# The last branch's keys turned and split inside the last attention instead of in the projection ahead of it

## The reference, cut to what matters

```python
for layer in range(DEPTH):
    x = sandwich(x, ..., swiglu, MACARON_WEIGHT)
    x = sandwich(x, ..., mixer, 1.0)
    x = sandwich(x, ..., swiglu, MACARON_WEIGHT)
```

```python
qc, kc, vc, ks, vs, kw, vw, gl, qd, kd, vd = split_cols(h @ w_in, CD_COLS)
o_c = g[:, :, 0] * o_cmp + g[:, :, 1] * o_slc + g[:, :, 2] * o_win
o_d = moba_attention(qd, kd, vd, rel_table[...])   # softmax(q k / 8 + bias by distance) v
return concatenate([o_c, o_d]) @ w_out
```

## Time and profile before

| | us |
|---|---|
| median of 3 runs (965.33 to 965.87) | 965.79 |
| the profiled execution, its own time | 966.07 |
| its span | 964.3 |
| TensorE busy | 957.3 (99%) |
| VectorE busy | 774.7 (80%) |
| ScalarE busy | 498.8 (52%) |
| GpSimd busy | 120.7 (13%) |
| granted TensorE clock | 1.00 in nearly all of the span |

### The profile page before, as it was taken

How to read it: one execution, slowest core, us unless ns; L and a number is a source line. 1 busy time by engine, 2 the same in 40 slices (tenths; PEclk the granted TensorE clock), 3 DMA queues, 4 the chain that set the end, 5 groups by cost and what they waited for, 6 DMA issues and landing times.

```text
span 964.3 us, 13463 instructions
## 1 busy us (share of the span) xinstructions
PE 957.3 (99%) x4670; PEld 810.3 (84%) x4670; DVE 774.7 (80%) x1471; ACT 498.8 (52%) x806; POOL 120.7 (13%) x129
## 2 busy tenths in 40 slices
PE   9999999999999999999999999999999999999997
PEld 8888888899888888888888888888889888888886
DVE  6789888768578988887898888878778588888884
ACT  6535343678464443445635353567667465343432
POOL 1200000166520000000200000022242420000000
PEclk9999999999999999999999999999999999999999
DMA  9875566242755657477085756527650436665631
GB/s 354 303 252 198 194 211 229 66 143 88 236 201 175 225 170 249 140 243 235 23 291 175 231 175 217 218 88 232 252 175 2 154 109 212 224 213 179 202 103 44
DMA packets 122178, 179.20 MB, mean 186 GB/s; under 512 B 3056, under 2 KB 97288, under 8 KB 121876
## 3 DMA queue, kind: packets, MB, share of 16 engines
q1 hardware_dynamic: 118900, 172.52, 53.2%
q10 hardware_dynamic: 2928, 4.98, 1.6%
q0 software_dynamic: 304, 1.09, 0.4%
HBM read 177.49 MB, written 1.09 MB: 185 GB/s over the span
## 4 chain that ended last, share of the span: by engine, by line
PE 97%; DVE 1%; issue 1%; ACT 1%; POOL 0%; DVEq 0%; POOLq 0%; ACTq 0%
PE ps L1329 93%; PE ps L1582 1%; PE ps L1367 1%; PE ps L1716 0%; DVE w_lo L1857 0%; PE ps L1343 0%; DVE down_lo L2354 0%; DVE end_hi L2159 0%; ACT moba_k L1313 0%; ACT logit L1124 0%; ACT gpost L1124 0%; PE ps L1442 0%; DVE down_lo L2150 0%; DVE xn L2165 0%; DVE x L1911 0%
## 5 line engine op out<-in xcount | busy, mean ns | idle before, releaser
L1329 PE MATMUL ps<-w_hi,xt_hi 128*128 128x512 f32 (+3 forms) x912 | 351.5, 388 | 0.0
L1329 PE MATMUL ps<-w_hi,xt_lo 128*128 128x512 f32 (+3 forms) x912 | 349.1, 386 | 0.0
L1329 PE MATMUL ps<-w_lo,xt_hi 128*128 128x512 f32 (+3 forms) x912 | 348.5, 385 | 0.0
L1857 DVE TENSOR_TENSOR w_lo<-raw,w_hi 128x2048 fp32r<-128x2048 f32 (+3 forms) x107 | 234.9, 2234 | 47.7 <-ACT w_hi L931 47.2
L1957 DVE STREAM_TRANSPOSE ps<-h 32x128 f32<-32x128 f32 x624 | 201.4, 323 | 9.2
L931 ACT ACTIVATE w_hi<-raw 128x2048 fp32r<-128x2048 f32 (+3 forms) x110 | 200.0, 1864 | 1.9 <-PE ps L1329 1.6
L1329 PEld LDWEIGHTS ps<-w_hi,xt_lo 128*128 128x128 f32 x912 | 171.4, 188 | 33.5
L1329 PEld LDWEIGHTS ps<-w_lo,xt_hi 128*128 128x128 f32 x912 | 171.6, 188 | 32.6
L1329 PEld LDWEIGHTS ps<-w_hi,xt_hi 128*128 128x128 f32 x912 | 171.3, 188 | 32.4
L1042 ACT ACTIVATE ht_hi<-ps 128x512 fp32r<-128x512 f32 x40 | 23.9, 598 | 285.2 <-DVE ps L1957 283.2
L1329 PE MATMUL ps<-down_hi,ht_hi 128*128 128x512 f32 x320 | 124.8, 390 | 0.0
(11 more groups left out here) (219 smaller groups left out, 843.3 us busy)
## 6 DMA issues: line engine op xcount, KB each, us to landing
raw<-in_l_ffn_wg SPq DMA_DIRECT2D x41, 1024.0 KB, 7.3
raw<-in_l_ffn_wu SPq DMA_DIRECT2D x41, 1024.0 KB, 9.8
raw_down<-in_l_ffn_wd SPq DMA_DIRECT2D x40, 1024.0 KB, 5.0
raw<-in_l_w_in SPq DMA_DIRECT2D x10, 1024.0 KB, 7.1
raw<-in_l_w_out SPq DMA_DIRECT2D x8, 1024.0 KB, 6.2
xn<-in_l_ffn_wd SPq DMA_DIRECT2D x4, 1024.0 KB, 7.3
raw<-in_l_w_in SPq DMA_DIRECT2D x4, 768.0 KB, 6.4
lead<-in_first SPq DMA_DIRECT2D x7, 384.0 KB, 6.1
```

Of the source, the lines that this page charges most:

```text
L1329: return pe.matmul(dst, lhs, rhs, start=start, stop=stop, skip_group_check=True)
L1857: dve.tensor_tensor(part(w_lo), part(raw), part(w_hi).bitcast(F32), ALU.subtract).then_inc(main_lo, 1)
```

## The change

The eight transposes of the keys leave chunk 5 of the projection. Four of them are made in step 14 (job 0) and four in step 18 (job 1), behind the scores of the step and ahead of its other transposes, both jobs in bank 6. Step 14's wait until slc tile 0 has been scaled out of that bank; step 18's wait until both low parts of job 0 have been read from it. ScalarE makes the high parts in steps 15, 16, 19 and 20, VectorE the low parts in steps 16, 17, 20 and 22, each behind the exponent or the logits and ahead of the step's copy. GpSimd adds the first two branches ahead of doubling the keys, and the other two behind. The scores of step 24 wait for the keys of job 0, those of step 28 for job 1. ScalarE's copy of the second tile of the values now comes directly behind the first exponents, and VectorE's scaling of the compressed heads directly behind the first logits. The waits that kept banks 0 and 1 until the keys were read are gone; the values of step 29 wait for the last low part.

```diff
+        KEYS_PE = {14: 0, 18: 1}
+        KEYS_ACT = {15: (0, 0), 16: (0, 1), 19: (1, 0), 20: (1, 1)}
+        KEYS_DVE = {16: (0, 0), 17: (0, 1), 20: (1, 0), 22: (1, 1)}
...
-                       job_base["kvv"]: 1, job_base["kd"]: 0, job_base["kd"] + 1: 1}
+                       job_base["kvv"]: 1, job_base["kd"]: 6, job_base["kd"] + 1: 6}
...
+                    add_branches(0, 2)
                     for i in range(2):
                         for par in range(2):
...
                             pool.wait_ge(moba_hi, 5 + 2 * i + par)
                             pool.tensor_copy(hi[others, :, :], hi[rows, :, :]).then_inc(moba_doubled, 1)
...
-                    add_branches()
+                    add_branches(2, 4)
...
-            for name, part, scale in (("qd", 0, scale_a), ("kd", 1, 1.0)):
-                if name == "kd":
-                    exps_ahead("slc")
...
+            def last_high(name, i, par):
+                job, rows = job_base[name] + i, slice(64 * par, 64 * par + 64)
+                act.wait_ge(t_ready, job + 1)
+                act.activation(moba_slots(i, par)[name == "kd"][rows, :, :], t_bank_two(job)[rows, :, :], ACT.Copy,
+                               scale=scale_a if name == "qd" else 1.0).then_inc(moba_hi, 1)
+            for i in range(2):
+                for par in range(2):
+                    last_high("qd", i, par)
+            exps_ahead("slc")
             project_out(j0 + 10, 4, lambda t: [(val[:, t, :], ps[:, 2 + t, :])], tiles=(1,))
-            exps("slc", ALL_STEPS - LAST_BASE)
+            exps("slc", ALL_STEPS - LAST_BASE, aside={n: lambda at=at: last_high("kd", *at) for n, at in KEYS_ACT.items()})
...
-                    if u == LAST_BASE + 4:
-
-                        pe.wait_ge(t_done, job_base["kd"] + 1)
-                    if (name, t, hh) == ("moba", 0, 0):
-                        pe.wait_ge(moba_doubled, 4)
-                        pe.wait_ge(moba_zeroed, 4)
+                    if name == "moba" and t == 0 and hh % 4 == 0:
+                        pe.wait_ge(t_done, job_base["kd"] + 1 + hh // 4)
+                        pe.wait_ge(moba_doubled, 2 + 2 * (hh // 4))
+                        pe.wait_ge(moba_zeroed, 2 + 2 * (hh // 4))
...
-                        if (name, t, hh) == ("win", 0, 0):
+                        if (name, t, hh) == ("moba", 0, 0):
 
                             pe.wait_ge(t_done, job_base["kd"] + 2)
...
-            def turn_last_keys():
-                pe.wait_ge(cmp_t_done, 2)
-                turn_four("kd", 512)
+            def turn_last_keys(i):
+                pe.wait_ge(head_out, OUT_AT["slc", 0])
+                turn_one_of_four("kd", 512, i)
...
-                    beside={3: scores_ahead, 5: turn_last_keys})
+                    beside={3: scores_ahead})
...
+            def last_low(i, par):
+                rows = slice(64 * par, 64 * par + 64)
+                _, k_hi, k_lo = moba_slots(i, par)
+                dve.wait_ge(moba_hi, 5 + 2 * i + par)
+                ins = dve.tensor_tensor(k_lo[rows, :, :], t_bank_two(job_base["kd"] + i)[rows, :, :],
+                                        k_hi[rows, :, :].bitcast(F32), ALU.subtract)
+                if par == 1:
+                    ins.then_inc(t_done, 1)
...
-                aside={5: lambda: compressed_out(1)})
+                aside={5: lambda: compressed_out(1), **{n: lambda at=at: last_low(*at) for n, at in KEYS_DVE.items()}})
```

More of the change, by code:

```diff
@@ L828, in split_both, with add_branches @@
                 split_low(n)
-            def add_branches():
-                for i, (name, t) in enumerate((("slc", 0), ("win", 0), ("slc", 1), ("win", 1))):
+            def add_branches(first, end):
+                for i in range(first, end):
+                    name, t = (("slc", 0), ("win", 0), ("slc", 1), ("win", 1))[i]
                     pool.wait_ge(head_out, OUT_AT[name, t])
@@ L1355, in turn_two, with turn_one_of_four @@
                            for i in range(2) for t in range(TILES)])
+            def turn_one_of_four(name, at, i):
+                turn_two(job_base[name] + i, lambda t, k: stage[:, t, at + (2 * i + k) * P:at + (2 * i + k + 1) * P])
             def turn_four(name, at):
                 for i in range(2):
-                    turn_two(job_base[name] + i, lambda t, k: stage[:, t, at + (2 * i + k) * P:at + (2 * i + k + 1) * P])
+                    turn_one_of_four(name, at, i)
             def turn_whole(src, t, name, before=lambda k: None):
@@ L1831, in _ @@
                          lambda kt, hh: val[:, kt, hh * HEAD:(hh + 1) * HEAD])},
-                LAST_BASE, ALL_STEPS - LAST_BASE, turned="out1")
+                LAST_BASE, ALL_STEPS - LAST_BASE, turned="out1",
+                aside={n: lambda i=i: turn_last_keys(i) for n, i in KEYS_PE.items()})
             pe.wait_ge(proj_out, OUT["w_in1"][3])
@@ L2339, in _ @@
                  32: lambda: scale("moba", 0, 512), 40: lambda: scale("moba", 1, 512)}, turned="out1",
-                aside={5: lambda: compressed_out(1)})
[L2341 to L2358, removed]
+                aside={5: lambda: compressed_out(1), **{n: lambda at=at: last_low(*at) for n, at in KEYS_DVE.items()}})
+            for i in range(2):
+                for par in range(2):
+                    rows, others = slice(64 * par, 64 * par + 64), slice(64 * (1 - par), 64 * (2 - par))
+                    q, _, _ = moba_slots(i, par)
+                    dve.wait_ge(moba_hi, 1 + 2 * i + par)
+                    ins = dve.scalar_tensor_tensor(q[others, :, :], t_bank_two(job_base["qd"] + i)[rows, :, :], scale_a,
+                                                   q[rows, :, :].bitcast(F32), ALU.mult, ALU.subtract)
+                ins.then_inc(t_done, 1)
+            dve.wait_ge(bias_landed, 16)
+            dve.wait_ge(d_lo, 6 * FBLOCKS)
+            first_last()
             compressed_out(0)
```

## The result

The changed kernel takes 968.18 us (median of 10 executions, 967.72 to 968.48) against 965.82 for the one before (10 executions beside it). The ratio is 1.0025, 95% interval 1.0017 to 1.0033: slower by 2.4 us, 0.25%. The profiled execution has a span of 966.7 us.

A forecast was written before the change was run, and what follows sets the result against it. TensorE bounds the kernel, with VectorE having little room beside it. The terms -1.24 + 0.36 + 0.80 + 0.59 + 0.67 + 0.68 + 0.52 give +2.38 us, so 968.2 from 965.79; range 966.5 to 969.2.

The forecast's parts named there:

- sign of being wrong: Wrong if TensorE has no gap at scores 18, or if the end of the attention comes before 753.3.
- The start: Start of the last attention: transposes leave TensorE's queue, scores of step 3 come earlier, 1.24 us won by step 13.
- The moved transposes: Steps 14 and 18: four key transposes each on TensorE, at half of 0.79 us, +0.80 in all.
- The wait for the bank: Step 14: transposes wait for VectorE to scale the selected branch's heads out of bank 6; TensorE waits 0.36 us.
- The subtractions: VectorE's four, 0.71 us each, delay copies; TensorE waits 0.59, 0.68 and 0.52 us before scores 18, 22 and 24.
- Cheaper in place: Rival: a subtraction among the steps lets the next instruction start sooner; at some 0.55 us, +1.8, 967.6; chance 0.11.
- Step 18: Step 18's transposes reuse bank 6 and wait 0.67 us for VectorE's second subtraction.
- the bounds: Limits, subtractions hidden or exposed: +0.5 or +3.4 us; hidden leaves some 0.56 in step 18 for ScalarE and bank.
- GpSimd's cover: GpSimd's adds and doublings are done in time for scores 24 and 28; a microsecond later still, nothing would wait.
- Hidden: Rival: VectorE's idle time absorbs the subtractions, so not slower; -0.1 up to +1.5 us, 965.7 to 967.3; chance 0.22.
- Faster: Rival: only the earlier start counts, the transposes being hidden in waits; -1.24 us, 964.6; chance 0.03.
- The clock: Rival: TensorE rests 2.8 us in ten, in pieces under 0.7, and its granted clock falls; chance 0.03.

The follow-up runs named there:

- The spread version: The change with the key work spread over other steps and each subtraction behind the step's copy of turned probabilities: 965.18 us against 965.78 for the kernel before.
- one column: The change with each of the four subtractions covering one column instead of 256 in both heads: 966.28 us against 965.78 for the kernel before.
- the run behind the copy: The change, same steps, with each subtraction behind the step's copy of turned probabilities instead of ahead of it: 968.03 us against 965.78 for the kernel before.

## Why the prediction was right

**What bounds the kernel: right.** TensorE was without gaps, so each wait put on it came through to the time. Neither sign of being wrong came: there is a gap at scores 18, and the attention ends at 754.26, not before 753.3.

**The start: right in kind, 0.3 too small.** Most of it is the term for the compressed values: their eight passes took 1.54 us to the next start (717.01 to 718.55) where 1.78 was reckoned, so the scores of step 3 came ahead even of the modelled end of that record (1.89 us long). The rest lies in steps 5 to 7, which came at 0.90 to 0.93 us apiece where before they took 0.92 to 0.98. I had left those as they were, because they wait for the first copies, and didn't see that VectorE's scaling of the compressed heads, which before stood behind the four subtractions (it started at 720.23, in the change at 718.07), had been what made these late. That this is the reason is an inference from the two timelines; no run takes it alone away.

**The moved transposes: 0.40 a job, measured 0.43 to 0.49.** The spread version has them without a wait: step 16 takes 1.35 us instead of 0.91. Half of the projection's 0.79 was too little.

**The wait for the bank: right** (0.36; 0.39 between the end of scores 14 and the transposes, counting 0.32 for the scores; shown by the run that turns in step 15).

**The subtractions: right, as to mechanism and place.** The runs with one column and with two of each show that most of the loss hangs on them: 1.56 us less at the attention's end without, 2.42 more with twice as many. Their size, 0.71, was right only on average. A subtraction on the lower half took 0.60, one on the upper 0.72 and started 0.1 late besides; with that 0.1 the four come to 0.72 on average. No full-width subtraction of any run took less than 0.59 from its start to the next instruction's (732.02 to 732.61 in the run behind the copy), so no run shows the 0.55 of "Cheaper in place"; the +1.8 and the 967.6 worked out from it were the author's estimate.

**Step 18: the term was half right.** It came out at 1.30 with its transposes, reckoned 1.07, and its cause is shared: with the subtractions as good as gone, ScalarE's copy in step 16 still held it for 0.6. The chain left that copy out; the bounds had it, with 0.56.

**GpSimd's cover: right for the change as it is.** No wait for it shows in these steps: its first two adds were done at 733.08 and its last doubling at 739.20 (reckoned 733.2 and 739.2), against scores 24 at 740.92 and 28 at 744.28. That it would have borne a microsecond more was not tried.

**Rivals.** "Hidden" fell with the wait of 0.30 at scores 18. "Cheaper in place" was half true (two of four at 0.60), without changing the side. "Faster" fell with the time. The clock stayed at 1.00 in the change, and the run with GpSimd's old order showed what it costs when it doesn't.

## What to carry to other kernels

In a pipeline written out by hand an instruction that fits an engine's idle time on average can still be late every time it matters: list, step by step, when each result is wanted, and put the moved work where the engine has caught up and behind what the others wait for. The same instructions cost 2.85 us less that way. And where the critical engine would wait long in one piece, as for the 2.45 us here, in which the clock went from 1.00 to 0.50, reckon with its clock as well as with the wait.

## What the runs showed of the hardware that was not expected

**The granted clock.** In the run with GpSimd's order of before, TensorE rested 2.45 us ahead of scores 24, from 739.55 to 742.00. The clock in that gap was 1.00 from 740.5 to 741.0, 0.82 from there to 741.5 and 0.50 to its end. From 742.0 to 758.0 TensorE was busy for 16.00 of 16.00 us and the clock stayed at 0.50; it was 0.61 from 758.0 to 758.5 and 1.00 from there to 759.0. In the run with each subtraction made twice, four shorter gaps within eleven us did not bring it down: it was 1.00 in each stretch of 5 us from 730 to 750. The gaps are the brackets of these rows:

```profile
733.24 0.50 PE L1334 MATMUL ps<-mix_k,end_hi 128*128 128x256 f32 x2 [0.90 <-DVE probt L2058]
...
735.00 0.63 PE L1348 MATMUL ps<-ident,xn 128*128 128x128 f32 x4 [1.26 <-DVE down_hi L2347]
...
739.92 0.51 PE L1334 MATMUL ps<-mix_k,end_hi 128*128 128x256 f32 x2 [0.96 <-DVE probt L2058]
...
742.99 0.33 PE L1334 MATMUL ps<-moba_k,down_lo 128*128 128x128 f32 x1 [1.05 <-DVE gpost L2058]
```

All four executions of the former lie between 974.6 and 976.8 us, with a mean granted clock of 0.990 to 0.995 (0.999 to 1.0 in the ten of the change), so it was low for longer in each of them. By the length of the rest alone the rows don't agree: here the clock was down 2 us into it (741.5), in the run behind the copy a gap of 1.50 left it at 1.00 (all of 730 to 750), and behind the last product of the kernel before, which ended at 958.79, it was still 1.00 at 962.6 and 0.50 from 963.0.

**VectorE and halves of the partitions.** (An instruction on all 128 partitions is counted with the lower half here.) An instruction of 512 columns followed by one on the same half of the partitions gave way after 0.59 to 0.62 us (lower to full, lower to lower, upper to upper); where the half changes it was 0.70 to 0.73 (lower to upper and upper to lower in the projection before the change, upper to full in the steps), and a copy ahead of an upper one, otherwise 0.34, took 0.45 (732.95 to 733.40 in the run behind the copy). So a change of half cost about 0.1 us in all these rows, and the four subtractions of the projection before the change, which alternate between the halves, took 2.85 us together (717.38 to the scaling's start at 720.23), 0.71 each. In the run with each subtraction made twice the two kinds stand side by side, upper to upper 0.62 and upper to full 0.72:

```profile
733.55 0.69 DVE L2345 TENSOR_TENSOR w_lo<-ps,moba_k 64x512 fp32r<-64x512 f32 x1
...
734.17 0.69 DVE L2347 TENSOR_TENSOR down_hi<-ps,moba_k 64x512 fp32r<-64x512 f32 x1
...
734.89 0.42 DVE L2058 COPY probt<-ps 128x256 f32<-128x256 f32 x1
```

The rows of these instructions all fit this; why it is so, they don't tell.
